# Memory attention by pairs of heads, and an earlier read of the overflow flag, in a two-block transformer kernel

## What is computed

```python
def _memory_cross_attention(h, mem_n, w_q, w_kv, w_o):
    q = (h @ w_q).reshape(B, S, MEM_HEADS, MEM_HEAD_DIM)        # 4 heads of 256
    kv = (mem_n @ w_kv).reshape(B, M, 2, MEM_HEADS, MEM_HEAD_DIM)
    k, v = kv[:, :, 0], kv[:, :, 1]
    s = jnp.einsum('bshd,bmhd->bhsm', q, k).astype(jnp.float32) * (MEM_HEAD_DIM ** -0.5)
    p = jax.nn.softmax(s, axis=-1).astype(h.dtype)
    o = jnp.einsum('bhsm,bmhd->bshd', p, v).reshape(B, S, D)
    return o @ w_o
...
for e in range(N_EXPERTS):                                      # first block
    h = jax.nn.silu(t @ w_gate[e]) * (t @ w_up[e])
    y = y + combine[:, e:e + 1] * (h @ w_down[e]).astype(jnp.float32)
```

## Time and profile before

| | |
|---|---|
| median of 3 runs | 1690.66 us (1688.22 to 1693.26) |
| profiled execution: its time, its span | 1693.55 us, 1692.2 us |
| mean granted TensorE clock | 0.988 |
| TensorE, VectorE, ScalarE, GpSimd busy | 94%, 55%, 41%, 33% |
| share of the chain that ended last | PE 70%, DMA 14%, DVE 8%, ACT 5%, issue 2% |
| mean of the transfers | 263 GB/s |

### The profile page before, as it was taken

The page is one execution under the profiler, slowest core; times in us unless marked ns, Lnnn a source line. Parts: engine busy times, 40 slices in busy tenths (PEclk is TensorE's granted clock), DMA queues, the critical chain, the costliest instruction groups (busy, mean ns, idle before and its releaser), DMA issues.

```text
span 1692.2 us, 23299 instructions
## 1 busy us (share of the span) xinstructions
PE 1589.5 (94%) x9505; PEld 1258.2 (74%) x9505; DVE 926.9 (55%) x1466; ACT 685.4 (41%) x1017; POOL 561.0 (33%) x323
## 2 busy tenths in 40 slices
PE   7999999999999897999899999999999779999997
PEld 5878754545454443888789999999999668888885
DVE  5765412111111012676443797688533988898886
ACT  6655311010101001575353444344444985555553
POOL 3212000000000001313031444343455987887860
PEclk9999999999999998999999999999999999999999
DMA  7435899999999998535253555555566019999993
GB/s 275 155 100 186 329 396 420 421 422 421 421 420 421 422 421 330 193 125 176 86 177 123 186 189 187 174 195 186 188 234 220 29 69 317 359 349 349 345 354 145
DMA packets 99344, 444.81 MB, mean 263 GB/s; under 512 B 11152, under 2 KB 19856, under 8 KB 57632
## 3 DMA queue, kind: packets, MB, share of 16 engines
q1 hardware_dynamic: 86256, 404.90, 64.0%
q0 software_dynamic: 11264, 33.60, 5.3%
q10 hardware_dynamic: 1712, 4.76, 0.7%
HBM read 435.26 MB, written 7.86 MB: 262 GB/s over the span
## 4 chain that ended last, share of the span: by engine, by line
PE 70%; DMA 14%; DVE 8%; ACT 5%; issue 2%; SPq 1%; POOL 0%; ACTq 0%; DVEq 0%
PE ps L653 11%; PE ps L471 11%; PE ps L1092 11%; PE ps L472 11%; PE ps L473 10%; PE ps L1085 7%; DMA fix<-in_w_up 5%; DMA big<-in_w_up 5%; PE ps L676 2%; DVE fix_parts L1123 2%; DMA hl<-in_w_up 2%; PE ps L1071 2%; DMA hl<-in_w_down 2%; PE ps L636 1%; ACT fix_parts L1954 1%
## 5 line engine op out<-in xcount | busy, mean ns | idle before, releaser
L2388 POOL TENSOR_TENSOR fix_parts<-fix,fix_parts 128x512 fp32r<-128x512 f32 x59 | 144.8, 2456 | 715.1 <-ACT fix_parts L1954 715.0
L473 PE MATMUL ps<-hh_parts,fix_parts 128*128 128x256 f32 x1120 | 317.7, 284 | 0.0
L1123 DVE TENSOR_TENSOR fix_parts<-fix,fix_parts 128x1536 fp32r<-128x1536 f32 (+1 forms) x84 | 171.4, 2040 | 112.1 <-ACT fix_parts L1954 109.8
L471 PE MATMUL ps<-hh_parts,fix_parts 128*128 128x256 f32 x768 | 219.9, 286 | 6.7 <-issue 5.8
L472 PE MATMUL ps<-hl_parts,fix_parts 128*128 128x256 f32 x768 | 218.3, 284 | 0.0
L473 PEld LDWEIGHTS ps<-hh_parts,fix_parts 128*128 128x128 f32 x1120 | 215.6, 193 | 0.0
L653 PE MATMUL ps<-big 128*64 128x512 f32 x784 | 198.1, 594 | 11.3 <-DMA big<-in_w_up 5.8
L1954 ACT ACTIVATE fix_parts<-fix 128x2048 fp32r<-128x2048 f32 x84 | 160.8, 1915 | 70.9 <-PE ps L1092 54.6
L653 PEld LDWEIGHTS ps<-big 128*64 128x64 f32 x784 | 68.7, 137 | 129.6 <-issue 128.8
L471 PEld LDWEIGHTS ps<-hh_parts,fix_parts 128*128 128x128 f32 x768 | 148.3, 193 | 8.0 <-issue 8.0
L653 PE MATMUL ps<-fix,big 128*64 128x512 f32 x528 | 143.4, 594 | 5.4 <-DMA fix<-in_w_up 3.1
(11 more groups left out here) (400 smaller groups left out, 3734.0 us busy)
## 6 DMA issues: line engine op xcount, KB each, us to landing
fix<-in_expert_u SPq DMA_DIRECT2D x64, 1024.0 KB, 5.3
fix<-in_expert_v SPq DMA_DIRECT2D x38, 1024.0 KB, 8.0
big<-in_w_up SPq DMA_DIRECT2D x35, 1024.0 KB, 23.8
big<-in_w_gate SPq DMA_DIRECT2D x33, 1024.0 KB, 20.5
big<-in_w_down SPq DMA_DIRECT2D x30, 1024.0 KB, 22.9
big<-in_expert_v SPq DMA_DIRECT2D x26, 1024.0 KB, 7.7
fix<-in_w_gate SPq DMA_DIRECT2D x23, 1024.0 KB, 21.6
fix<-in_w_down SPq DMA_DIRECT2D x22, 1024.0 KB, 23.0
```

What stands on the lines that cost most here:

```text
L471: pe.matmul(o, l[0], r[0], start=first, stop=False)
L473: return pe.matmul(o, l[1], r[0], start=False, stop=last)
L1123: nc.vector.tensor_tensor(m.fr(x[:, 0:end]), x[:, 0:end], m.fr(hi[:, 0:end]).bitcast(F32), ALU.subtract).then_inc(s.lo_v, 1)
L2388: nc.gpsimd.tensor_tensor(m.fr(x[:, at:2048]), x[:, at:2048], m.fr(hi[:, at:2048]).bitcast(F32), ALU.subtract).then_inc(s.lo_g, 1)
```

## The change

It has two parts.

**Pairs of heads.** Four units, 12 to 15, of two heads each take the place of two of four. Each has one PSUM bank. Units 12 and 13 are heads 0 and 1 of token blocks 0 and 1, and need the first half of the query alone; 14 and 15 are heads 2 and 3. The scores, the softmax, the transposes and the copies of 12 and 13 are put between the pieces of `qm1`. Units 14 and 15 and the turn of Y, now in two halves, are put between the pieces of the output product. That product first takes the upper half of its rows (h = 0) for both halves of its columns, then the lower. Its weights' rows are held in chunks of 128 consecutive ones (`tile_by_chunk`, `BY_CHUNK`) so that a half of the rows belongs to two heads. Copies of the probabilities: VectorE for token block 0, ScalarE for block 1, one of 512 columns a unit.

**The flag.** The functions of the first block for TensorE, ScalarE and VectorE become generators. They stop ahead of expert pair 14, where the three engines read the flag; the branch stays behind pair 15. SyncE and GpSimd neither wait for it nor read it.

```diff
-BY_CHUNK = ("outf", "outd", "outa")
-TURN_BANK = {"outd": 4}
+BY_CHUNK = ("outf", "outd", "outa", "memo")
+TURN_BANK = {"outd": (4, 5), "memo": (0, 2, 1, 3)}
...
-UNITS += [dict(j=3, b=b, g=0) for b in (0, 1)]
+UNITS += [dict(j=3, b=b, g=g) for g in (0, 1) for b in (0, 1)]
...
+BEATSM = {0: [("MS", 12), ("MS", 13)], 1: [("ME", 12), ("ME", 13), ("MR", 12), ("MR", 13)], 2: [("MC", 12), ("MC", 13)]}
...
+def pe_mem_scores(pe, m, s, u):
+    b, h0, bank, _, _ = mem_unit(m, u)
+    for x in range(2):
+        for c in range(2):
+            k = 2 * (h0 + x) + c
+            ins = pe.matmul(m.PS[:, bank, 256 * x:256 * x + 256], m.QM[:, k, b * P:(b + 1) * P], m.KM[:, k, :],
+                            start=(c == 0), stop=(c == 1))
+    ins.then_inc(s.att_s, 1)
...
+        if g == 14:
+            yield
...
+    features("qm0", f["w_qm"], m.HT, "cross")
+    features("qm1", f["w_qm"] + 2, m.HT, "cross", 0, BEATSM)
...
+    for u in (12, 13):
+        pe_mem_mix(pe, m, s, u)
+    pe.wait_ge(s.out_v, after["qm1"][0])
+    pe_mem_scores(pe, m, s, 14)
+    pe.wait_ge(s.att_o, 14)
+    pe_turn(pe, m, s, m.Y, "memo", (0, 4))
+    pe_mem_scores(pe, m, s, 15)
+    om(0, 0, 0)
+    for u in (14, 15):
+        pe_mem_turn(pe, m, s, u)
+    om(0, 0, 1)
+    for u in (14, 15):
+        pe_mem_mix(pe, m, s, u)
+    om(0, 1, 0)
+    pe.wait_ge(s.att_o, 16)
+    pe_turn(pe, m, s, m.Y, "memo", (4, 8))
+    om(0, 1, 1)
     for i in range(2):
-        pe_product(pe, m, s, t, f"om{i}", f["w_om"] + 2 * i, (6, 4)[i], before, m.HT, "memo", beat, None)
+        for b in range(2):
+            om(1, i, b)
...
+    features("qm1", f["w_qm"] + 2, m.QM[:, 4:8], 1.0 / 16, None, 0, BEATSM)
+    for u in (12, 13):
+        dve_mem_mixed(u)
+    dve_mem_max(14)
+    dve_turn(nc, m, s, "memo", None, m.HT[1], m.HT[0], (0, 4))
+    dve_mem_max(15)
+    for u in (14, 15):
+        dve_mem_copy(u)
+    tile = f["w_om"]
+    low(tile)
+    for u in (14, 15):
+        dve_mem_mixed(u)
+    low(tile + 1)
+    dve_turn(nc, m, s, "memo", None, m.HT[1], m.HT[0], (4, 8))
...
+    product(f["w_qm"] + 2, 0, BEATSM)
+    act_turn(nc, m, s, "memo", None, m.HT[0], (0, 4))
+    for u in (14, 15):
+        act_mem_exps(u)
+    for u in (14, 15):
+        act_mem_copy(u)
+    high(f["w_om"])
+    high(f["w_om"] + 1)
+    act_turn(nc, m, s, "memo", None, m.HT[0], (4, 8))
...
-    po.wait_ge(s.flag, 1)
...
-    sy.wait_ge(s.flag, 1)
...
-    value = nc.values_load(m.flag[0:1, 0:1], min_val=0, max_val=8192)
...
+    for first in firsts:
+        next(first)
+    surplus = nc.values_load(m.flag[0:1, 0:1], (mybir.EngineType.PE, mybir.EngineType.Activation, mybir.EngineType.DVE), min_val=0, max_val=8192)
+    for first in firsts:
+        next(first, None)
+    overflow(nc, a, m, s, surplus)
```

More of the change, by code:

```diff
@@ L374, in weight_tiles @@
     add("w_qm", product(a["w_q_mem_2"][0], 0, 512))
-    add("w_om", product(a["w_o_mem_2"][0], 0, 512))
+    add("w_om", [tile_by_chunk(a["w_o_mem_2"][0], h, n0) for h in range(2) for n0 in (0, 512)])
     add("w_query", product(a["w_query_2"][0], 0, 512, 1024, 1536))
@@ L923, in beat @@
                 ins.then_inc(s.row_mm, 1)
+            elif what == "MS":
+                if u == 12:
+                    pe.wait_ge(s.kv_in, 48)
+                    pe.wait_ge(s.out_v, after["qm0"][0])
+                    pe.wait_ge(s.turn_lo, turned("cross", 7))
+                pe_mem_scores(pe, m, s, u)
+            elif what == "MR":
+                pe_mem_turn(pe, m, s, u)
             elif what == "peerturn":
@@ L987, in tensor_second @@
     pe_turn(pe, m, s, m.X, "cross")
-    for i in range(2):
-        features(f"qm{i}", f["w_qm"] + 2 * i, m.HT, "cross")
-    pe.wait_ge(s.turn_lo, turned("cross", 7))
-    pe.wait_ge(s.out_v, after["qm1"][0])
-    pe.wait_ge(s.kv_in, 48)
-    for u in (12, 13):
-        b, b0 = UNITS[u]["b"], 2 * PLACES[u]
-        S4 = m.PS[:, b0:b0 + 2, :].rearrange("p a (c k) -> p (a c) k", k=256)
-        for h in range(4):
-            for c in range(2):
-                ins = pe.matmul(S4[:, h, :], m.QM[:, 2 * h + c, b * P:(b + 1) * P], m.KM[:, 2 * h + c, :],
-                                start=(c == 0), stop=(c == 1))
-        ins.then_inc(s.att_s, 1)
@@ L1275, in dve_rope, with vector_first @@
     v.step(ve.tensor_tensor(x2, m.RT[2], m.RT[3], ALU.add))
-def vector_first(nc, m, s, t, before, after):
+def vector_first(nc, m, s, t, before, after, settled):
     ve = nc.vector
@@ L1378, in vector_first @@
     dve_router(nc, m, s, t, v)
-    return dve_experts(nc, m, s, t, v)
+    yield from dve_experts(nc, m, s, t, v)
+    settled.append(v.n)
 def dve_group(nc, m, s, name, parts, out, j):
@@ L1401, in dve_half_out, with dve_add @@
             ve.scalar_tensor_tensor(xb, m.PS[:, out_banks(name)[i] + b, :], rstd[:, b:b + 1], xb, ALU.mult, ALU.add).then_inc(s.out_v, 1)
-def dve_add(nc, m, s, t, i, tile):
+def dve_add(nc, m, s, t, i, last):
     ve = nc.vector
@@ L1407, in dve_add @@
         xb = m.X[:, b, 512 * i:512 * i + 512]
-        ve.wait_ge(s.used, t.used[tile + 1] - 1 + b)
+        ve.wait_ge(s.used, t.used[last] - 1 + b)
         ve.tensor_tensor(xb, xb, m.PS[:, (6, 4)[i] + b, :], ALU.add).then_inc(s.out_v, 1)
@@ L1552, in dve_experts @@
         hb = m.HB[g % 2]
+        if g == 14:
+            ve.wait_ge(s.flag, 1)
+            yield
         if g == 0:
@@ L1639, in beat @@
                 dve_mixed(nc, m, s, v, u)
+            elif what == "ME":
+                dve_mem_max(u)
+            elif what == "MC":
+                dve_mem_copy(u)
             elif what == "conv" and u == 0:
@@ L2015, in act_mixed_sq, with scalar_first @@
                          accum_out=oss8[:, n:n + 1]).then_inc(s.att_q, 1)
-def scalar_first(nc, a, m, s, t, before, after):
+def scalar_first(nc, a, m, s, t, before, after, kvkeep, settled):
     ac = nc.scalar
@@ L2178, in scalar_first @@
             ac.wait_ge(s.kv_kept, 32)
+        if g == 14:
+            ac.wait_ge(s.flag, 1)
+            yield
         ac.wait_ge(s.used, t.used[tile + 3])
@@ L2219, in high, with act_mem_exps, act_mem_copy @@
             act_high(nc, m, s, t, t.split[tile] + AHEAD)
+    def act_mem_exps(u):
+        b, h0, bank, pm, _ = mem_unit(m, u)
+        ac.wait_ge(s.att_m, u + 1)
+        for x in range(2):
+            h = h0 + x
+            ins = ac.activation(pm[:, x, :], m.PS[:, bank, 256 * x:256 * x + 256], ACT.Exp, bias=m.nms[b][:, h:h + 1],
+                                scale=rs[:, b:b + 1], accum_out=m.lsums[b][:, h:h + 1])
+        ins.then_inc(s.att_e, 1)
+    def act_mem_copy(u):
+        b, _, bank, _, pt = mem_unit(m, u)
+        if b:
+            ac.wait_ge(s.att_r, blocks_before(12)[0] + u - 11)
+            ac.activation(pt, m.PS[:, bank, :], ACT.Copy).then_inc(s.att_ta, 1)
     def beat(i, beats=BEATS2):
```

162 lines of the change are left out of this document (77 added, 85 removed).

## The result

The changed kernel takes 1680.51 us (median of 6 runs, 1677.41 to 1683.31), the kernel before 1691.33 us beside it (6 runs, 1688.22 to 1693.26): ratio 0.9931, 95% interval [0.9920, 0.9942], faster by 10.8 us by the medians. Two later comparisons of the same two kernels gave 0.9945 [0.9927, 0.9962] and 0.9941 [0.9922, 0.9960]. The direction was right, and so was the place where the time was to be won; the gain was forecast at 6.7 us and is 9 to 12 by the three ratios.

The account below looks back on a forecast made before the run. TensorE, busy 94% of the span, was taken as the bound, with 7.2 us of handshake holes in the memory attention. 7.2 - 0.7 = 6.5, plus 0.2 for the flag, took 1690.66 to 1684.0 us, range 1680.0 to 1689.5.

Parts of the forecast that it names:

- The five holes: TensorE's waits around the memory attention, from before the scores to before the output product: all covered, 7.19 us.
- The net cost of the cuts: Inserted pieces cut TensorE's product stream: 5 more cuts cost 0.7 to 1.25 us, taken as 0.7 for overlapping tails.
- The slacks: Spare time at attention handshakes: 0.5 us at the second unit's transposes, the tightest; every other above 0.6 us.
- The flag: Read moved ahead of expert pair 14: saves 0.2 us; the stall follows the branch, not the read.
- What lies behind the attention: Stages after the memory attention hang on TensorE's products and start earlier by the same time, with no further gain.
- one stretch at half clock, more or fewer: As TensorE's stalls shift, about 2.3 us either way if as long as the 4.85 us one; inside the range.
- The sum: Whole kernel: 6.5 us from the attention plus 0.2 from the flag, 6.7 us, median 1684.0 us.
- The rivals: Handshakes leak (chance 0.16), late read was the stall (0.08), gain given back later (0.03), slower by the conversion chain (0.04).
- The late read was the stall: Behind the last scatter, TensorE starts at 668.2; whole gain 8 to 10 us, 1681 to 1682.6 us; chance 0.08.

Follow-up runs that it names:

- pairs_only: Changed kernel with the flag read put back in its old place for all five engines; ratio 0.9953 to the kernel before.
- behind: Changed kernel with attention units 12 and 13 put behind the whole second query product instead of between its pieces; ratio 0.9964 to the kernel before.
- ahead: Changed kernel with units 14 and 15 and both turns in one block ahead of the output product; ratio 0.9939 to the kernel before.
- no_branch: Changed kernel without the surplus tokens' code and the branch around it, flag read kept; ratio 0.9931 to the kernel before.
- short_body: Changed kernel with the surplus code behind the same branch cut from 32 experts to one; ratio 0.9908 to the kernel before.

## Why the prediction was right or wrong

- **The five holes (7.2 us): right.** TensorE's idle time from the query product to the turn ffn2 falls from 7.98 to 0.78 us, by 7.20. pairs_only shows that the attention alone does it, behind and ahead that it is the place of the small pieces: with the pairs kept and the cover gone, holes are back.
- **The net cost of the cuts (0.7 us, "as holes also shorten by the matmuls' overlapping tails"): the step that failed inside the attention.** The net was taken as a loss and is a gain of 1.0: without that idle time the stage fell from 66.23 us (74.21 - 7.98) to 65.25 (66.03 - 0.78). It has two parts. Measured from start to start, scores went from 7.14 to 6.54 us (3.27, 1.72, 1.54), transposes from 2.03 to 1.74, mixes from 7.07 to 6.72, the output's turn from 2.06 to 1.67: 1.6 us less, since a piece that had a hole behind it now has its last matmuls overlapped by what follows. The products, cut into pieces, gave 0.7 back (the output product 22.60 for 22.02, the query product 23.35 for 23.27), about what the prediction took for the cuts. So the cut was priced nearly right and the overlap was the term that was mis-sized: it was named, given no size, and is more than twice the cost. ahead shows both from the other side. Attention: 8.2 us instead of 6.5.
- **The slacks: right in place, too wide in size.** The second unit's transposes had nearly nothing to spare instead of 0.5 us; the second half of the turn at 843.46 had 1.85 us behind VectorE's last scaling (841.61) where 2.1 were forecast. No handshake leaked, no product waited for a split.
- **The flag (0.2 us): right that it is next to nothing, its size not measured.** The difference of 0.1 us between two traces is far inside what executions differ by; the branch record did not shrink. The choice between the read and the branch as the cause, made from VectorE's row, was confirmed by no_branch and short_body.
- **What lies behind the attention ("starts earlier by the same time"): the step that failed outside it.** It was 3.2 us shorter in the profile. The prediction had put one stretch at half clock, more or fewer, at 2.3 us inside its range; a stretch behind these stalls measures 1.1 to 1.5 us, but three stages changed at once: the activations by 1.1 us and the last loads by 1.5, with one stretch fewer each, and the one-hot products by 0.6. Over 14 profiles with the new attention this time is 823.4 us on average (821.50 to 825.79), over four with the old one 826.5 (825.90 to 827.92). The two groups do not overlap. That one kernel's executions differ by up to 3.3 us here is shown; why the old order had 825.9 us or more four times in four and the new one never is open.
- **The sum.** The traces show 8.2 us in the attention and at most 0.1 for the flag, where 6.7 were forecast. The rest of the 9 to 12 us measured answers to the time behind the attention, about 3 us less on average in the profiles. By the medians the first comparison (10.8 us) has 2.5 us beyond the 8.3, the second (8.7) 0.4 and the third (12.4) 4.1.
- **The rivals.** None happened. "The late read was the stall" names 1681 to 1682.6 us, close to the time measured, by a mechanism that the trace refutes: that is luck, not support for it.

## What to carry to other kernels

Count a covered hole at its full length and then add the overlap that the work ahead of it gains (1.6 us over five holes here); the cuts between independent pieces cost less than that (0.7 us). Before a stall behind a branch is put down to the value that it tests, look at its length on another engine, and try a short body: if it is the jump, a hint some instructions ahead hides it. And when a change shifts a kernel's later stages, give the stalls there a two-sided term of their own: each may win or lose one or two stretches at half clock, 1.1 to 1.5 us apiece here, that no instruction accounts for.

## What the runs showed of the hardware

- TensorE's record of a taken branch over a long body is 5.2 to 6.4 us in all fourteen profiles of that kind here, over a short body 0.37, with a hint 0.49. VectorE's record is 0.07 us each time, and yet its next instruction comes 2.9 us later than its last one ended with the long body (3.8 with the read) and within 0.3 (short body) or 0.65 us (hint). The record of a branch is thus no measure of its stall.
- One stall of 3.0 us was followed by 6.8, 3.4 or 0 us at the lower clock, in executions that differ in nothing around it. "TensorE: Matmul & The Clock Gate" in the Trainium skill, section "What's actually happening", says that the number of matmuls at the lower clock varies from run to run at a kernel's start. The rows show such a variation at stalls inside a kernel, at 1.1 to 1.5 us for each stretch of 3.4.
- The one-hot products go the other way. Their stage, from the stall ahead of them to the one ahead of the last loads, takes 74.0 to 74.2 us in the six profiles whose clock stays at 1.00 behind the first of these stalls, and 73.5 to 73.6 in the twelve where it is at half for 3.4 us. TensorE's idle time inside the stage is 19.2 to 19.5 us in the six and 14.7 to 16.0 in the twelve, so the stage is not paced by TensorE's clock. All six have a stretch at half clock behind the second stall too; of the twelve, three have. No run here explains the link. The two stalls in the kernel before (clock 1.00, then 0.53 behind them) and after (0.56, then 1.00):

```profile
1308.89 2.39 PE L1071 MATMUL ps<-hh 128*128 128x128 f32 x16 [2.50 <-POOL hh L2430]
1382.93 0.77 PE L1085 MATMUL ps<-fix_parts,big_parts 128*128 128x512 f32 x1 [2.24 <-DVE big_parts L1798]
```

```profile
1301.02 3.38 PE L1118 MATMUL ps<-hh 128*128 128x128 f32 x16 [2.49 <-POOL hh L2516]
1374.50 0.47 PE L1132 MATMUL ps<-fix_parts,big_parts 128*128 128x512 f32 x1 [2.25 <-DVE big_parts L1868]
```
